# Half of the frequencies, with even and odd tokens apart, in the filters' spectrum, in Fourier and in Hyena, and another order of Hyena and Fourier

## What is computed

```python
def fourier_mixer(u):
    ug = u.reshape(B, L, FNET_GROUPS, -1).astype(jnp.float32)
    y = jnp.fft.fft2(ug, axes=(1, 3), norm='ortho').real
    return y.reshape(B, L, -1).astype(u.dtype)

def long_conv(z, hf, hb, skip):
    k = jnp.concatenate([hf, jnp.zeros((1, C), hf.dtype), hb[1:][::-1]], axis=0)
    zf = jnp.fft.rfft(z, n=2 * L, axis=1)
    kf = jnp.fft.rfft(k, axis=0)
    y = jnp.fft.irfft(zf * kf[None], n=2 * L, axis=1)[:, :L]
    return y + skip * z

def hyena_mixer(u, p):
    v, x1, x2 = jnp.split(u_c, 3, axis=-1)
    h = hyena_filters(u.shape[1], p)
    z = v
    for n, gate in enumerate((x1, x2)):
        z = gate * long_conv(z, h[:, n, 0], h[:, n, 1], skip[n])
    return z.astype(u.dtype)
```

## Time and profile before

| | |
|---|---|
| median of 3 runs | 1892.24 us |
| the profiled execution | 1892.72 us, span 1890.9 us |
| TensorE busy | 1770.3 us (94%) |
| VectorE busy | 861.3 us (46%) |
| ScalarE busy | 621.6 us (33%) |
| GpSimd busy | 103.7 us (5%) |
| granted TensorE clock, mean | 0.955 of full |
| front, to the first projection | 0 to 88.6 us |
| projections | 88.6 to 196 us |
| mixing without attention | 196 to 310.3 us |
| attention | 310.3 to 381 us |

### The profile page before, as it was taken

How to read it: one execution, slowest core, us unless ns; L and a number is a source line. 1 busy time by engine, 2 the same in 40 slices (tenths; PEclk the granted TensorE clock), 3 DMA queues, 4 the chain that set the end, 5 groups by cost and what they waited for, 6 DMA issues and landing times.

```text
span 1890.9 us, 20524 instructions
## 1 busy us (share of the span) xinstructions
PE 1770.3 (94%) x8201; PEld 1407.7 (74%) x8201; DVE 861.3 (46%) x1196; ACT 621.6 (33%) x813; POOL 103.7 (5%) x137
## 2 busy tenths in 40 slices
PE   8999688899999889999999698998998899999997
PEld 3478465778887668888878577997886788888886
DVE  3553335657666454444433534312664543333223
ACT  1442114832222233333322253323553332223221
POOL 1000200010101000000000100000432000000000
PEclk9999897999999889999999698999999999999998
DMA  9232100154445323333233121222110233332331
GB/s 331 80 126 79 45 0 1 45 182 165 154 146 179 111 67 89 90 97 97 77 92 106 50 88 50 66 68 91 47 46 23 67 90 89 103 98 68 92 98 54
DMA packets 214165, 172.40 MB, mean 91 GB/s; under 512 B 5428, under 2 KB 202932, under 8 KB 214070
## 3 DMA queue, kind: packets, MB, share of 16 engines
q1 hardware_dynamic: 207222, 145.85, 25.7%
q0 software_dynamic: 6848, 25.23, 3.9%
HBM read 168.94 MB, written 2.13 MB: 90 GB/s over the span
## 4 chain that ended last, share of the span: by engine, by line
PE 86%; DVE 8%; ACT 4%; issue 1%; DMA 0%; DVEq 0%; SPq 0%; ACTq 0%
PE PS L426 22%; PE PS L427 21%; PE PS L428 21%; PE PS L435 4%; PE PS L1831 2%; PE PS L550 2%; PE PS L914 2%; DVE WL L91 1%; PE PS L444 1%; DVE T L91 1%; PE PS L445 1%; PE PS L446 1%; ACT WH L87 1%; DVE X L102 1%; DVE SQ L102 1%
## 5 line engine op out<-in xcount | busy, mean ns | idle before, releaser
L426 PE MATMUL PS<-XH,WH 128*128 128x512 f32 (+1 forms) x1280 | 492.6, 385 | 5.9 <-DVE WL L91 4.3
L427 PE MATMUL PS<-XL,WH 128*128 128x512 f32 (+1 forms) x1280 | 492.9, 385 | 0.0
L428 PE MATMUL PS<-XH,WL 128*128 128x512 f32 (+1 forms) x1280 | 490.8, 383 | 0.0
L91 DVE TENSOR_TENSOR WL<-WS,WH 128x2048 fp32r<-128x2048 f32 (+1 forms) x129 | 272.4, 2111 | 269.9 <-ACT WH L87 269.3
L426 PEld LDWEIGHTS PS<-XH,WH 128*128 128x128 f32 x1280 | 241.9, 189 | 60.2 <-DVE WL L91 4.4
L427 PEld LDWEIGHTS PS<-XL,WH 128*128 128x128 f32 x1280 | 241.7, 189 | 49.0
L428 PEld LDWEIGHTS PS<-XH,WL 128*128 128x128 f32 x1280 | 241.8, 189 | 48.8
L87 ACT ACTIVATE WH<-WS 128x2048 fp32r<-128x2048 f32 (+1 forms) x129 | 228.6, 1772 | 78.6 <-PE PS L428 61.8
L426 PE MATMUL PS<-HH,WH 128*128 128x512 f32 x352 | 137.3, 390 | 2.1 <-DVE WL L91 2.0
L427 PE MATMUL PS<-HL,WH 128*128 128x512 f32 x352 | 137.1, 390 | 0.0
L428 PE MATMUL PS<-HH,WL 128*128 128x512 f32 x352 | 137.1, 389 | 0.0
(11 more groups left out here) (325 smaller groups left out, 2463.8 us busy)
## 6 DMA issues: line engine op xcount, KB each, us to landing
WS<-in_w_in SPq DMA_DIRECT2D x24, 1024.0 KB, 5.2
WS<-in_ffn_w_up SPq DMA_DIRECT2D x44, 512.0 KB, 4.9
WS<-in_ffn_w_in SPq DMA_DIRECT2D x44, 512.0 KB, 4.9
MSRC<-in_w_mod POOLq DMA_DIRECT2D x32, 512.0 KB, 4.3
WS<-in_fox_w_in SPq DMA_DIRECT2D x16, 1024.0 KB, 5.6
WS<-in_ffn_w_down SPq DMA_DIRECT2D x16, 704.0 KB, 4.6
WS<-in_ffn_w_out SPq DMA_DIRECT2D x16, 704.0 KB, 4.6
MODW<-in_w_mod SPq DMA_DIRECT2D x8, 1024.0 KB, 10.3
```

The costliest lines, as they stand in the source:

```text
L91: self.e.tensor_tensor(o, a, b, op).then_inc(*self.done.to(*key))
L426: e.matmul(o, lh, rh, start=first and i == 0, stop=False)
L427: e.matmul(o, lh, rl, start=False, stop=False)
L428: ins = e.matmul(o, ll, rh, start=False, stop=last and i == n - 1)
```

## The change

The spectrum, Fourier's second step and both directions of Hyena's transform use that cosines and sines at frequency L - f are those at f with the sign of the odd tokens turned. Tokens are taken with the even ones first and the odd ones behind; the sums over even and over odd tokens are made apart, for the lower half of the frequencies, and their sum and difference give both halves.

- The spectrum: four rounds with two products each, an even and an odd one of two matmuls; ScalarE copies the even one, VectorE adds and subtracts the odd one. The table is half as large.
- `lo_chunk` of the first projection's weights moves ahead of the mods on VectorE; `hi_chunk` ahead of the norm on ScalarE; the sum of |h| goes behind the spectrum's halves and the second `lo_chunk`.
- Mixing: Fourier's first step in four banks of its own; then Hyena's first transposes and forward products; then Fourier's second step and pooling; then Hyena's backward products. Forward and backward have two blocks of frequencies. VectorE does halves, products and the fold for j = 1; GpSimd the fold for j = 0 (for both orders), Fourier's sum and difference, and then `bias_pool`, which stood ahead of all this. Q's and K's remainders go behind Hyena's first products, in two parts.
- Two tables (DF, DB) of 1 MB in place of DM, both awaited ahead of the first forward product.
- The load of the first gate chunk waits for Hyena's last product, since the products' buffers lie in its slot; the bias's load goes ahead of it.
- The gate reads the backward sums of even and odd tokens from two banks, alternating.

```diff
     def spectrum_pe(e, i):
         j, kind = divmod(i, 2)
...
+        if i >= 2:
+            e.wait_ge(*acts.at("spectrum", i - 2))
+        if i == 3:
+            e.wait_ge(*dve.at("norm1", "scaled", 7))
+        for odd in range(2):
+            prod32(e, bank((EVEN, ODD)[odd][i]), [(FC[:, s, kind, 128 * j:128 * j + 128], (FP, FM)[kind][:, s, :])
+                                                  for s in (2 * odd, 2 * odd + 1)], ("spectrum", i, odd))
...
+    def spectrum_dve(v, i):
+        j, kind = divmod(i, 2)
+        K = (KR, KI)[kind]
+        v.e.wait_ge(*acts.at("spectrum", i))
+        v.e.wait_ge(*pe.at("spectrum", i, 1))
+        v.tt(K[:, j, :], K[:, 2 + j, :], bank(ODD[i]), ALU.add)
+        v.tt(K[:, 2 + j, :], K[:, 2 + j, :], bank(ODD[i]), ALU.subtract, key=("spectrum", i))
...
     def front_dve(v):
         diagonal_dve(v, "norm1", L)
+        lo_chunk(v, PROJ)
         mod_dve(v)
...
-        lo_chunk(v, PROJ)
+        for i in range(4):
+            spectrum_dve(v, i)
+        lo_chunk(v, PROJ + 1)
         for p in range(4):
             e.wait_ge(*acts.at("filt_abs", p))
...
+    def hy_back_pe(e, n, j):
+        if j == 0:
+            e.wait_ge(*pool.at("hy_times", n))
+        else:
+            e.wait_ge(*dve.at("hy_times", n))
+        for cb in range(2):
+            for q in range(2):
+                for kind in range(2):
+                    ins = e.matmul(bank(3 + 2 * cb + q, 256), YP[:, j, q, 256 * kind + 128 * cb:256 * kind + 128 * cb + 128],
+                                   DB[:, j, q, kind, :], start=j + kind == 0, stop=j + kind == 2)
...
     def mix_pe(e):
...
+        for n in range(2):
+            if n == 0:
                 e.wait_ge(*dve.at("four_c", 0))
             else:
                 e.wait_ge(*dve.at("hy_gated", 0, 1))
+            hy_turn_pe(e, n)
             if n == 0:
+                e.wait_ge(*acts.at("proj", 21))
+                e.wait_ge(*landed("hy_tables", 2))
+                e.wait_ge(*dve.at("four_c", 3))
+            e.wait_ge(*dve.at("hy_turned", n, 0))
+            e.wait_ge(*acts.at("hy_turned", n, 1))
+            for j in range(2):
+                hy_forward_pe(e, n, j)
+            if n == 0:
+                e.wait_ge(*landed("four_l"))
+                for fb in range(2):
+                    for q in range(2):
+                        prod32(e, bank(FOUR[fb][q], 256),
+                               [(AB[:, tb, fb, 128 * x:128 * x + 128], CLS[:, tb, 256 * x:256 * x + 256])
+                                for tb in (2 * q, 2 * q + 1) for x in range(2)], ("four_l", fb, q))
+                e.wait_ge(*landed("pool_wd"))
+                e.wait_ge(*dve.at("hy_halves", 0, 0))
...
+                e.wait_ge(*acts.at("four_odd", 1))
+            for j in range(2):
+                hy_back_pe(e, n, j)
...
+    def hy_times_dve(v, n, j):
+        e = v.e
+        z = ZS[j]
+        e.wait_ge(*acts.at("hy_even", n, j))
+        e.wait_ge(*pe.at("hy_forward", n, j, 1))
+        odd = bank(FORWARD[j][1])
+        v.tt(z[:, 0, :], z[:, 1, :], odd, ALU.add)
+        v.tt(z[:, 1, :], z[:, 1, :], odd, ALU.subtract, key=("hy_halves", n, j))
+        for K, o in ((KR, ZA), (KI, ZB)):
+            k = K[:, j:j + 3:2, 256 * n:256 * n + 256].unsqueeze(2).broadcast_to([128, 2, 2, 256])
+            v.tt(o[:, :, :].rearrange("p h (x c) -> p h x c", x=2), z[:, :, :].rearrange("p h (x c) -> p h x c", x=2), k,
+                 ALU.mult)
+        v.tt(z[:, :, 0:256], ZA[:, :, 0:256], ZB[:, :, 256:512], ALU.subtract)
+        v.tt(z[:, :, 256:512], ZA[:, :, 256:512], ZB[:, :, 0:256], ALU.add, key=("hy_product", n, j))
...
+    def mix_pool(g):
+        g.e.wait_ge(*dve.at("hy_product", 0, 0))
+        hy_fold(g, 0, 0, ("hy_times", 0))
+        for fb in range(2):
+            even, odd = T[fb][:, 0:256], T[2][:, 256 * fb:256 * fb + 256]
+            g.e.wait_ge(*acts.at("four_odd", fb))
+            g.tt(T[fb][:, 256:512], even, odd, ALU.subtract)
+            g.tt(even, even, odd, ALU.add, key=("four_y", fb))
+        bias_pool(g)
+        g.e.wait_ge(*dve.at("hy_product", 1, 0))
+        hy_fold(g, 1, 0, ("hy_times", 1))
...
     def mix_dve(v):
...
+            for j in range(2):
+                hy_times_dve(v, n, j)
+            hy_fold(v, n, 1, ("hy_times", n))
+            if n == 0:
+                for m in range(2):
+                    e.wait_ge(*acts.at("y_hi", m))
+                    v.stt(YL[:, m, :], bank(m), vec("pool_scale", m), YH[:, m, :].bitcast(F32), ALU.mult,
+                          ALU.subtract, key=("y_lo", m))
+                for fb in range(2):
+                    e.wait_ge(*acts.at("y_hi", 2 + fb))
+                    v.tt(YL[:, 2 + fb, :], T[fb][:, :], YH[:, 2 + fb, :].bitcast(F32), ALU.subtract,
+                         key=("y_lo", 2 + fb))
+                qk_lo_dve(v, 0)
+            else:
+                qk_lo_dve(v, 1)
                 e.wait_ge(*acts.at("kc_hi"))
...
+                y = PS[:, 1024 * cb + 1536:1024 * cb + 2560].rearrange("p (q t) -> p t q", q=2)[:, 0:256, :]
...
+                ot = o.rearrange("p (t q) -> p t q", q=2)
+                v.stt(ot, y, SM[:, c:c + 1], ot, ALU.mult, ALU.add)
```

More of the change, by code:

```diff
@@ L700, in front_act @@
         root_act(a, "norm1", L)
+        hi_chunk(a, PROJ)
         for k in range(8):
             normed_act(a, "norm1", k, SQ[:, k, 0:L], XH[:, k, 0:L], modcol(0, k))
[L703 to L711, removed]
+            if k in (1, 3, 5):
+                spectrum_act(a, k // 2)
+        spectrum_act(a, 3)
+        hi_chunk(a, PROJ + 1)
+        for p in range(1, 4):
+            filt_abs_act(a, p)
     def front_pool(g):
@@ L771, in proj_pe @@
             else:
+                if i == 1:
+                    e.wait_ge(*acts.at("spectrum", 2))
                 for n in (2 * i, 2 * i + 1):
@@ L871, in mix_pe, with hy_turn_pe @@
+    def hy_turn_pe(e, n):
+        src = HV if n == 0 else Z1
+        for q in range(2):
+            for x in range(4):
+                h, cb = x // 2, x % 2
+                ins = e.transpose(bank(3 + q, 128, off=128 * x), src[:, cb, part(h, q)], ID[:, :])
+            ins.then_inc(*pe.to("hy_turned", n, q))
     def mix_pe(e):
         e.wait_ge(*landed("four_c"))
-        e.wait_ge(*acts.at("proj", 21))
+        e.wait_ge(*dve.at("filt_norm"))
         for tb in range(4):
-            if tb == 3:
-                e.wait_ge(*dve.at("four_c", 0))
[L877 to L896, removed]
+            for fb in range(2):
+                ins = e.matmul(bank(4 + tb, 256, off=256 * fb), FU[:, fb, part(tb % 2, tb // 2)], CC[:, :],
+                               start=True, stop=True)
+            ins.then_inc(*pe.to("four_c", tb))
+        for n in range(2):
+            if n == 0:
+                e.wait_ge(*dve.at("four_c", 0))
             else:
@@ L935, in mix_act @@
             split_act(a, K1H[m][:, :], K1[:, m, :], ("k_hi", m))
[L936 to L955, removed]
+        hy_act(a, 1)
+        e.wait_ge(*dve.at("y_lo", 3))
+        hy_skip_act(a, 1)
         a.act(KCH[:, :, :], KC[:, :, :], ACT.Copy, key=("kc_hi",))
+        e.wait_ge(*pe.at("hy_forward", 1, 1, 1))
         a.act(VHN[:, 2:6, :], V1[:, :, :], ACT.Copy, key=("v_hi", 0))
@@ L964, in mix_dve, with qk_lo_dve @@
+    def qk_lo_dve(v, m):
+        for hi, lo, full, what in ((Q1H, Q1L, Q1, "q_hi"), (K1H, K1L, K1, "k_hi")):
+            v.e.wait_ge(*acts.at(what, m))
+            v.tt(lo[:, m, :], full[:, m, :], hi[m][:, :].bitcast(F32), ALU.subtract, key=("qk_lo", m))
     def mix_dve(v):
         e = v.e
-        for m in range(2):
-            for hi, lo, full, what in ((Q1H, Q1L, Q1, "q_hi"), (K1H, K1L, K1, "k_hi")):
-                e.wait_ge(*acts.at(what, m))
-                v.tt(lo[:, m, :], full[:, m, :], hi[m][:, :].bitcast(F32), ALU.subtract, key=("qk_lo",))
```

180 lines of the change are left out of this document (95 added, 85 removed).

## The result

The changed kernel takes **1846.68 us** (median of four runs, 1845.88 to 1847.53) where the kernel before takes 1892.33 (1892.21 to 1893.19): a ratio of 0.9758, with a 95% interval of 0.9741 to 0.9775. The forecast was 1847.5. The profiled execution took 1847.53 us.

The account below looks back on a forecast made before the run. TensorE held 86% of the chain, with VectorE the bound in mixing once products are halved. 1892.7 - 9.7 (front) + 2.8 (clock) - 37.8 (mixing) = 1848.0, median 0.5 lower: 1847.5 us, own range 1839 to 1856.

Parts of the forecast that it names:

- Front: Spectrum to second projection: 13.7 us of matmuls go, a 4.6 us wait ahead of filt_norm appears, 9.7 us gained.
- The clock's charge of 2.8: TensorE: 2.8 us lost to a lower clock after each idle of over 4 us, ends 0 to 3.2.
- Rival (D): Projections behind filt_norm: the gap ahead of it leaves TensorE at the lower clock, about 1940 us; chance 0.03.
- Tables: Mixing, ahead of Hyena's first forward products: tables land 9.0 us after the projections' end, a 4.4 us wait.
- First order: Mixing, Hyena's first order: VectorE becomes the bound, gate done 46.2 us from the projections' end, before 75.6.
- The hold by GpSimd: Mixing, first order: VectorE held 1.2 us by GpSimd's fold, 2.6 by Fourier's sums, 2.2 by the first bias addition.
- Rival (A): Mixing: GpSimd and VectorE don't hold each other up and the clock stays high, 1828.6 us; chance 0.15.
- TensorE's wait for the gate: Mixing, ahead of the second transposes: TensorE idles some 9 us until VectorE's gate releases it.
- Second order: Mixing, Hyena's second order: attention starts 76.5 us from the projections' end, before 114.3; 37.8 us gained in mixing.
- The two-bank read and the strided weights: Gate's PSUM read and TensorE's even/odd weight reads: taken at 0; otherwise 0.75 to 1.5 us per gate read, 0.2 per matmul.
- rival (B): VectorE's path longer: tables at 10.5, every idle at 3.2 us, two-bank read doubled, 1854.7 us; chance 0.18.
- rival (C): Whole change: GpSimd's and VectorE's added work eats the halves, time within 0.2% of before; chance 0.02.

Follow-up runs that it names:

- e2: Changed kernel with the sum of |h| done a block at a time between the spectrum's halves, the second chunk's remainder behind both: 1836.97 us.
- e1: Changed kernel with GpSimd's bias addition moved ahead of its wait for the projections' end and the tables' load: 1841.2 us.
- e9: Changed kernel with early bias addition, the sum of |h| between the spectrum's halves and a semaphore for each table, together: 1830.42 us.
- e3: Changed kernel with each of the spectrum's matmuls done twice, as many as before the change: 1855.08 us.
- e7: Changed kernel with every matmul of Fourier's second step and of Hyena's forward and backward products done twice: 1864.04 us.
- e4: Changed kernel with unused matmuls put into TensorE's four waits, as added work: 1839.98 us.

## Why the prediction held, and where its terms were off

- **Front, right.** The wait ahead of filt_norm came where it was forecast: sum of |h| at 90.5 (90.0), idle 4.96 (4.6). The clock's charge of 2.8 was 3.0: filt_norm 0.9 longer, and from there to the end of the projections another 2.1, by e2, which lacks the wait. Against the kernel before, the same 2.1 (8.4 sooner at the second projection, 6.25 at their end) is in part luck. A second low stretch came (0.59 from 120 to 124 us), behind an idle of 2.76 us that the kernel before has too and after which its clock stayed at 1.00; and an idle of 1.48 us that it had later is gone. Rival (D) fell: the clock was back at 0.80 of full from 96 to 98 us and at 1.00 from 98 to 100.
- **Tables, right, by two errors that cancel.** 8.9 us from the projections' end (9.0). The sum left out that the first load is issued only 0.42 us behind that end (190.17, and 196.42 before), and counted the second issue in full (0.75). The last byte landed 8.5 us behind the first issue, where one load of 2 MB took 8.3, so the second issue cost 0.2:

```profile
DF<-in_hy_forward POOLq DMA_DIRECT2D x1, 1024.0 KB, 5.9
DB<-in_hy_back POOLq DMA_DIRECT2D x1, 1024.0 KB, 7.7
```

- **First order, mechanism right, sizes off.** The forward half took VectorE to 14.4 us (15.4): the charge for the clock there was 1.8, not 2.8. The hold by GpSimd was sized too large: 12.3 us in the sum, 11.1 of them in the first order. By the rows, 0.98 + 0.40 + 0.81 + 2.17 = 4.4 up to the end of the fold (forecast 6.0) and 1.7 + 1.7 = 3.4 behind it (5.1). By what held VectorE, GpSimd's fold cost 0.98 (forecast 1.2), Fourier's sums 1.6 (2.6; 0.41 of it lies in the 2.17), and the bias additions 1.8, 1.7 and 1.7 (2.2 each), one of them lying under the pair from PSUM. The sum charged whole instructions of GpSimd, and VectorE is held only for what is left of one (the two rows of 218 us above). Rival (A) prices the same hold at 13.7, which the terms, 12.3 with the second order, don't give. The gate was done at 42.6 instead of 46.2. The Trainium skill, "SBUF — State Buffer", section "Who interferes with whom", has it that a VectorE instruction with a single input in SBUF stays out of the blocking; the 1.60 for two with the bias addition beside them, and the same 1.60 in e1 without it, now show that half too. TensorE's wait for the gate was 7.76 us (8.9).
- **Second order.** 31.8 us instead of 30.3: the forward half was 2.5 longer for the clock (I had 1.9), and each gap between instructions a little more than nothing. With the first order, attention's VectorE work starts at 74.35 us from the projections' end instead of 76.5: 40.0 us gained in mixing (37.8).
- **The two-bank read and the strided weights** cost nothing (0.75 us; the transposes took 1.11 us where the clock was up, 1.09 before), so rival (B) fell; SyncE's load of the gate chunk was issued at 253.3 and waited for by nobody.
- **Missed.** Attention took 74.3 us instead of 71.4 in these two executions, 2.9 us that were in no term. They go with a clock that stays low longer; that the change caused it isn't shown (see e9). Behind attention 1.9 us came back that I can't place. Front +0.65, mixing -2.15, attention +2.9, the rest -1.9: from 1848.0 to the measured 1847.5, so part of the closeness is luck: errors that cancel.
- Rival (A) fell by the stretched instructions and by e1, rival (C) by e3 and e7: doubling the work again brings the time back by 8.4 and 17.4 us. That is not all of the 45.7: the forecast has the idle of 8.62 us that goes by another order in it too, and no run tested that part.

## What to carry to other kernels

When a product is halved, look at once for what the engine will wait for next, and in whose queue that stands: here a sum with nothing to do with the product stood behind it on VectorE, and moving it between the halves was worth 9.7 us (8.7 by the traces), as much as the halved spectrum brought (8.4). GpSimd work with no deadline belongs where VectorE is idle: 9.8 us of bias addition in the wrong place cost 5.5. Give each of two transfers its own semaphore if their readers are apart; 4.8 us for two changed lines.

## What the runs showed of the hardware

- Idle TensorE costs clock when it starts again. After 4.96 us of idle the clock stood at 0.50 from 90 to 96 us; after 4.40 the forward products took 8.83 us, after 1.83 and 0.30 the same products took 7.15 and 7.17, with the clock at its upper level. How long an idle may last isn't settled: behind 2.40 us the clock fell to 0.50 (e3, from 104 to 106 us), and behind the same 2.76 us of idle in the projections it stayed at 1.00 in the kernel before and fell to 0.59 in the changed one. Unused matmuls in the waits were worth 6.7 us of 1847 (e4).
- A VectorE instruction with both inputs in SBUF, started while GpSimd reads SBUF, ended 0.55 us (512 elements) or 1.08 us (1024) behind the end of GpSimd's; those with one input in PSUM kept their time (1.41 and 1.60 for two).
- Attention, which no kernel here changes, took between 71.4 and 74.4 us in the twelve profiled executions, by when the clock rises in it. Whether that goes with the kernel or with the execution is open; a forecast of a few us for one stage has that much uncertainty from the stages behind it.
